# Three attention stages: transposes one block later, a third numerator tile, a joining DMA, and low parts made on GpSimd

## The reference, cut to what matters

```python
# first block: three dilations, joined by their log-sum-exps (one softmax with a mask of counts)
s = einsum('bhrnqe,bhrnke->bhrnqk', qb, kw); s = where(mask, s, NEG_INF)
p = exp(s - max(s)); o = einsum('bhrnqk,bhrnke->bhrnqe', p, vw) / sum(p)
# second block, twice (8 query heads, 2 key heads), then gated
scores = einsum('bqkgd,bskd->bkgqs', qb, k) * scale
y_attn = einsum('bkgqs,bskd->bqkgd', softmax(scores), v) * silu(g_a)
y = concatenate([y_attn, y_conv, y_four]) @ w_out[l]
```

## Time and profile before

| | |
|---|---|
| median of three runs | 3447.35 us |
| profiled execution, its time and its span | 3444.82 us, 3443.0 us |
| busy share of the span: PE, DVE, ACT, POOL | 95%, 60%, 39%, 12% |
| first attention, first scores to first projection matmul | 1203.45 to 1411.67 us |
| second | 2534.60 to 2743.55 us |
| third | 3137.11 to 3344.65 us |

### The profile page before, as it was taken

One profiled execution on the slowest core, in us unless ns is written; L12 is line 12 of the kernel. 1 busy time (PEld: TensorE's weight loads), 2 busy tenths in 40 slices (PEclk: granted clock), 3 DMA queues, 4 the chain that ended last, 5 costly groups with the idle time before them and its releaser, 6 DMA issues. The chain is left out here.

```text
span 3443.0 us, 39579 instructions
## 1 busy us (share of the span) xinstructions
PE 3274.5 (95%) x16006; PEld 2689.4 (78%) x16006; DVE 2076.9 (60%) x2647; ACT 1329.9 (39%) x1996; POOL 404.7 (12%) x505
## 2 busy tenths in 40 slices
PE   5999999999999789999999999899989999998998
PEld 3788888878797678878888888767868887786887
DVE  7555555554764789565655555562259886225986
ACT  4222222232334378432222222552147754214772
POOL 0000011121012112021011101001001200100120
PEclk8999999999998699999999999999999999999999
DMA  5222222226355368312222222224333312433331
GB/s 198 86 90 82 86 86 74 87 73 112 111 196 179 69 88 96 77 37 90 94 98 86 74 89 95 57 73 136 103 81 62 58 41 96 134 105 81 65 55 61
DMA packets 137366, 315.19 MB, mean 92 GB/s; under 512 B 55152, under 2 KB 72304, under 8 KB 126176
## 3 DMA queue, kind: packets, MB, share of 16 engines
q1 hardware_dynamic: 74960, 213.60, 19.6%
q0 software_dynamic: 62224, 99.05, 13.9%
HBM read 261.52 MB, written 51.10 MB: 91 GB/s over the span
## 5 line engine op out<-in xcount | busy, mean ns | idle before, releaser
L2088 DVE TENSOR_TENSOR w_lo<-w_raw,w_hi 128x1024 fp32r<-128x1024 f32 (+1 forms) x131 | 221.9, 1694 | 333.9 <-ACT w_hi L1502 333.9
L848 PE MATMUL psum<-a_hi,w_hi 128*128 128x512 f32 x704 | 276.5, 393 | 5.9 <-DVE a_lo L2210 3.8
L848 PE MATMUL psum<-a_hi,w_lo 128*128 128x512 f32 x704 | 274.9, 391 | 0.0
L848 PE MATMUL psum<-a_lo,w_hi 128*128 128x512 f32 x704 | 274.9, 390 | 0.0
L1256 PEld LDWEIGHTS psum<-mats,attn_num 128*128 128x128 f32 x1536 | 169.6, 144 | 115.4 <-ACT attn_num L1853 89.9
L1844 ACT ACTIVATE attn_th<-psum 128x512 fp32r<-128x512 f32 x384 | 209.6, 597 | 123.9 <-PE psum L1256 117.8
L2563 DVE TENSOR_TENSOR attn_tl<-psum,attn_th 128x512 fp32r<-128x512 f32 x384 | 247.2, 684 | 16.1 <-ACT attn_th L1844 12.1
L1256 PE MATMUL psum<-mats,attn_num 128*128 128x128 f32 x1536 | 215.3, 284 | 39.0 <-ACT attn_num L1853 28.8
L2278 DVE SCALAR_TENSOR_TENSOR x<-psum,cols,x 128x1024 f32<-128x1024 f32 x144 | 184.4, 1282 | 94.8 <-PE psum L848 94.6
L1502 ACT ACTIVATE w_hi<-w_raw 128x1024 fp32r<-128x1024 f32 (+1 forms) x131 | 183.8, 1403 | 143.0 <-PE psum L848 51.1
L2557 DVE TENSOR_REDUCE attn_sm<-psum 128x1 f32<-128x1024 f32 x128 | 156.0, 1220 | 32.0 <-PE psum L1246 31.9
(11 more groups left out here) (567 smaller groups left out, 8446.8 us busy)
## 6 DMA issues: line engine op xcount, KB each, us to landing
w_raw<-in_w_ada SPq DMA_DIRECT2D x52, 1024.0 KB, 5.0
w_raw<-in_w_gu SPq DMA_DIRECT2D x44, 1024.0 KB, 4.9
w_raw<-in_w_in SPq DMA_DIRECT2D x34, 1024.0 KB, 5.1
w_raw<-in_w_down SPq DMA_DIRECT2D x22, 1024.0 KB, 5.0
w_raw<-in_w_out SPq DMA_DIRECT2D x12, 1024.0 KB, 7.9
qk_hi_scratch<-p_out_hi POOLq DMA_DIRECT2D x18, 512.0 KB, 3.0
qk_lo_scratch<-p_out_lo POOLq DMA_DIRECT2D x18, 512.0 KB, 3.8
w_early<-in_w_ada SPq DMA_DIRECT2D x8, 1024.0 KB, 18.2
```

What stands on the lines that cost most here:

```text
L848: mm = e.matmul(bank, a[:, k * width + m * P:k * width + (m + 1) * P], b(k, h), start=(ends[0] and k == order[0] and i == 0), stop=(ends[1 ...
L2088: e.tensor_tensor(like(src, lo), src, like(src, hi.bitcast(F32)), ALU.subtract).then_inc(*w_done.mark(n, part))
```

## The change

1. **One more block in flight.** PE transposes block u-2 in iteration u and not u-1; ACT's `num_high`, DVE's `low_parts` and the product with the values move by one too; the loops run one iteration longer. The first attention gets a third numerator tile and a third tile for the maximum.
2. **The join of result halves.** For z < 14, ACT copies all 128 partitions of the product out of PSUM, and POOL issues an accumulating DMA that adds one half of 64 partitions onto the other (128 KB, SBUF to SBUF). POOL's multiplication reads its result. ACT's next-but-one copy waits for that multiplication, and PE's product waits for the copy and not for DVE's addition. DVE adds only for z = 14 and 15.
3. **Low parts on GpSimd.** The low parts of the first three pairs of heads, of `out1` block 1 and of the two ungated `out2` blocks are subtracted by POOL; ACT rounds those weights in four pieces of 512 columns (u = 16 to 19, and 32 to 35).
4. SP issues the two gated `out2` loads at z = 11 and not at z = 4.

```diff
-        a.sm = rings(f"{name}_sm", 2, [P, 1], F32, scope)
+        a.sm = rings(f"{name}_sm", 2 if between else 3, [P, 1], F32, scope)
-        a.tm = [t.sqh[i][0:64, :] for i in range(2)]
+        a.tm = [t.sqh[i] for i in range(2)]
+        if between is None:
+            a.nu.append(sb(f"{name}_num2", [P, S], F32, scope))
...
+    def low_by_pool(n):
+        return plan[n][3] in (("out1", 1), ("out2", 0, 0), ("out2", 0, 1), ("out2", 1, 0), ("out2", 1, 1))
+    def joined_by_dma(z):
+        return z < A_HEADS * ST // 4 - 2
...
@@ tensor_program, times_v and the loop
-                        e.wait_ge(*res_done.at(name, z - 2))
+                        e.wait_ge(*half_res.at(name, z - 2))
-            for u in range(n + 3):
+            for u in range(n + 4):
-                if 1 <= u < n + 1:
-                    turn_over(u - 1)
-                if u >= 3:
-                    times_v((u - 3) // 2, 1 - u % 2)
+                if 2 <= u < n + 2:
+                    turn_over(u - 2)
+                if u >= 4:
+                    times_v((u - 4) // 2, u % 2)
...
-                        e.wait_ge(*mix_lo.at(name, "ab"[k // 4], k % 4))
+                        e.wait_ge(*(mix_lo.at(name, "b", k % 4) if k // 4 else low_heads(name, k)))
...
@@ scalar_program
+        def high_piece(n, j):
+            if j == 0:
+                e.wait_ge(*landed(n))
...
+            c = slice(j * BLK // 4, (j + 1) * BLK // 4)
+            e.activation(part_split(n, 0)[0][:, c], raw_of(n)[:, c], ACT.Identity)...
         def round_weights(n, part):
+            if low_by_pool(n):
+                return
...
-                    e.wait_ge(*res_done.at(name, z - 2))
-                e.activation(a.tm[z % 2], ps.of[(name, "o")].half[z % 2][64:128, :], ACT.Identity)...
+                    e.wait_ge(*og_scaled.at(name, z - 2))
+                if joined_by_dma(z):
+                    e.activation(a.tm[z % 2], ps.of[(name, "o")].half[z % 2], ACT.Identity)...
...
-            for u in range(n + 4):
-                if u >= 7 and (u - 7) % 4 == 0:
-                    half_result((u - 7) // 4)
-                if 1 <= u < n + 1:
-                    num_high(u - 1)
+            for u in range(n + 5):
+                if u >= 8 and u % 4 == 0:
+                    half_result(u // 4 - 2)
+                if 2 <= u < n + 2:
+                    num_high(u - 2)
...
+                if 16 <= u < 20 and not masked:
+                    high_piece(blocks.index[tag + (0,)], u - 16)
+                if 32 <= u < 36:
+                    high_piece(blocks.index[tag + (1,)], u - 32)
...
@@ vector_program
-                    if u >= 2:
-                        e.wait_ge(*num_turned.at(name, u - 2, 1))
+                    if u >= len(a.nu):
+                        e.wait_ge(*num_turned.at(name, u - len(a.nu), 1))
...
-                if u >= 29 and (u - 29) % 16 == 0 and u < n:
-                    heads_low((u - 29) // 16)
...
@@ gpsimd_program, attention
+                if u >= 8 and u % 4 == 0 and joined_by_dma(u // 4 - 2):
+                    z = u // 4 - 2
+                    own, other = ((slice(0, 64), slice(64, P)), (slice(64, P), slice(0, 64)))[(z // 2) % 2]
+                    e.wait_ge(*half_res.at(name, z))
+                    e.dma_start(a.tm[z % 2][own, :], a.tm[z % 2][other, :], accum_op=ALU.add).then_inc(
+                        *halves_in[z % 2].mark(name, z))
                 if u >= 12 and u % 4 == 0:
...
-                    e.wait_ge(*res_done.at(name, z))
+                    e.wait_ge(*halves_in[z % 2].at(name, z))
                     e.wait_ge(*inv_in[z % 2].at(name, z))
...
-                    e.tensor_tensor(part, part, a.rs[z % 2][64 * hh:64 * hh + 64, :], ALU.mult)...
+                    e.tensor_tensor(part, a.tm[z % 2][of, :], a.rs[z % 2][of, :], ALU.mult)...
...
+                if u >= 32 and (u - 32) % 16 == 0 and u <= n:
+                    pp = (u - 32) // 16
+                    e.wait_ge(*og_scaled.now())
+                    e.wait_ge(*mix_hi.at(mix, "a", pp))
+                    e.tensor_tensor(m.mixa[1][:, pp, :], a.og[pp % 2][:], m.mixa[0][:, pp, :].bitcast(F32),
+                                    ALU.subtract).then_inc(*heads_lo.mark(mix, pp))
+                if u == 22 and gated:
+                    low_weights((tag[0], tag[1], 0))
+                if u == 38:
+                    low_weights(tag + (1,))
+        def low_weights(tag):
+            n = block_at(tag)
+            hi, lo = part_split(n, 0)
+            e.wait_ge(*og_scaled.now())
+            e.wait_ge(*w_hi.at(n, 0))
+            e.tensor_tensor(lo, raw_of(n), hi.bitcast(F32), ALU.subtract).then_inc(*w_low.mark(n))
...
@@ sync_program, attention
-                if gated and z == 4:
+                if gated and z == 11:
                     weights(first_block(("out2", i - 1, 0)) + 2 * RAW)
```

More of the change, by code:

```diff
@@ L688, in program_of @@
     og_scaled, og_gated, summed_g = (signal(n, "Pool") for n in ("og_scaled", "og_gated", "summed_g"))
+    w_low, heads_lo = (signal(n, "Pool") for n in ("w_low", "heads_lo"))
+    halves_in = loaded("halves_joined", "POOL", 2)
     const_in, x_in = signal("const_in", "SP", 16), loaded("x_in", "SP", 2)
@@ L787, in halves_of, with block_at, split_done, low_heads @@
         return part_split(n, 0)
+    def low_by_pool(n):
+        return plan[n][3] in (("out1", 1), ("out2", 0, 0), ("out2", 0, 1), ("out2", 1, 0), ("out2", 1, 1))
+    def block_at(tag):
+        return next(b for b, entry in enumerate(plan) if entry[3] == tag)
+    def split_done(n):
+        return w_low.at(n) if low_by_pool(n) else w_done.at(n)
+    def low_heads(mix, pp):
+        return heads_lo.at(mix, pp) if pp < A_HEADS // 2 - 1 else mix_lo.at(mix, "a", pp)
+    def joined_by_dma(z):
+        return z < A_HEADS * ST // 4 - 2
     def with_sums(n, part):
@@ L1493, in scalar_program @@
         blocks = Blocks(plan, lambda n, part: round_weights(n, part), lambda layer, i: None)
+        def high_piece(n, j):
+            if j == 0:
+                e.wait_ge(*landed(n))
+                if part_before[n, 0] is not None:
+                    e.wait_ge(*tile_done.at("block", *part_before[n, 0]))
+            c = slice(j * BLK // 4, (j + 1) * BLK // 4)
+            e.activation(part_split(n, 0)[0][:, c], raw_of(n)[:, c], ACT.Identity).then_inc(
+                *w_hi.mark(n, 0, *(() if j == 3 else (j,))))
         def round_weights(n, part):
+            if low_by_pool(n):
+                return
             if plan[n][0] == "w":
@@ L1829, in half_result @@
                 if z >= 2:
[L1830 to L1831 removed]
+                    e.wait_ge(*og_scaled.at(name, z - 2))
+                if joined_by_dma(z):
+                    e.activation(a.tm[z % 2], ps.of[(name, "o")].half[z % 2], ACT.Identity).then_inc(*half_res.mark(name, z))
+                else:
+                    e.activation(a.tm[z % 2][0:64, :], ps.of[(name, "o")].half[z % 2][64:128, :],
+                                 ACT.Identity).then_inc(*half_res.mark(name, z))
             def heads_high(pp):
@@ L2573, in results @@
                 e.wait_ge(*half_res.at(name, z))
-                if z % 4 == 0 and pp >= 2:
-                    e.wait_ge(*mix_lo.at(mix, "a", pp - 2))
                 e.tensor_tensor(a.og[pp % 2][64 * hh:64 * hh + 64, (z % 2) * HALF:(z % 2 + 1) * HALF],
-                                ps.of[(name, "o")].half[z % 2][0:64, :], a.tm[z % 2], ALU.add).then_inc(*res_done.mark(name, z))
+                                ps.of[(name, "o")].half[z % 2][0:64, :], a.tm[z % 2][0:64, :], ALU.add).then_inc(*res_done.mark(name, z))
             def heads_low(pp):
@@ L2612, in attention @@
                     ml_drained(e)
-                if u >= 7 and (u - 7) % 4 == 0:
-                    results((u - 7) // 4)
-                if 1 <= u < n + 1:
-                    low_parts(u - 1)
+                if u >= 8 and u % 4 == 0:
+                    if not joined_by_dma(u // 4 - 2):
+                        results(u // 4 - 2)
+                if 2 <= u < n + 2:
+                    low_parts(u - 2)
                 if u >= 4 and u % 4 == 0 and u <= n:
                     inverse_sums(u // 4 - 1)
-                if u >= 29 and (u - 29) % 16 == 0 and u < n:
-                    heads_low((u - 29) // 16)
                 if u == ST:
@@ L3086, in load_mix, with attention @@
                 e.dma_start(m.t[k][:], d.mix[first + k]).then_inc(*mix_in[k].mark(name, k))
-        def attention(name, mix, m, first, n_kv, gated):
+        def attention(name, mix, m, first, n_kv, gated, tag):
             a = m.at
@@ L3179, in block2 @@
             row(m.gain, d.gain[l], "gain", l)
-            attention(at_name, mix, m, 4, 2, True)
+            attention(at_name, mix, m, 4, 2, True, ("out2", l))
             e.wait_ge(*og_gated.now())
```

36 lines of the change are left out of this document (23 added, 13 removed).

## The result

The changed kernel takes 3392.2 us, the median of 4 runs (3388.0 to 3396.5), beside 3448.0 for the kernel before in the same session: a ratio of 0.984, with a 95% interval of 0.9823 to 0.9857. The profiled execution took 3396.5 us (span 3394.7), 48.3 less than that of before.

What follows compares the result with a forecast made beforehand. PE was taken to bound the kernel, waiting each block on ACT's exponential. Savings of 24.7, 22.4 and 17.7 us (64.8), less 6 for keys, gave 59: 3386 from 3444.8, stated as 3387, range 3377 to 3410.

Steps and rivals of the forecast that it cites:

- The ring: Attentions: transposes, high parts, exponential, transposes close a 2.93 us loop (2.96 in the first); an extra block gives 2.82.
- The splits: Five weight-block splits inside the attention loops stop all engines; removing them saves 7.4, 5.2 and about 6 us for three.
- the row that I costed them from: Second attention: three periods around a weight-block split take 16.16 us and not 8.8, so 7.4 us are lost.
- The join: POOL's accumulating DMA of result halves: free if it lands within 19.8 us, as ACT's copy waits for the multiplication.
- my 7 us for it: Gated stages: the accumulating DMA's landing, taken from the nearest load on the same queue, about 7 us.
- by that the join would be free everywhere: All attentions: with a fixed DMA cost of about 2 us, the accumulating DMA would cost nothing.
- Keys of the first attention: Keys take 12.6 us with 11.3 left, so PE waits 1.3 us at four of six loads: 6 us back.
- rival (a): First attention: queue bounds it, keys wait through values, join and multiplication; 19 us in place of 6, 3400; chance 0.22.
- (b): Attentions: period stays at 2.93 us for another reason, only splits and ends go; 3411 us; chance 0.12.
- (c): All attentions: joins land late and ACT's copy waits for POOL; at 25 us landing, 3495 us; chance 0.04.

Runs made afterwards that it cites:

- the undone version: The changed kernel with the weight blocks split by ACT and DVE inside the loop again, out2 loads at z = 4: 3425.7 us, 0.9932.
- block_only: The kernel before plus only the extra block in flight and the third tile: 3417.8 us, 0.9914.
- mult_behind: The changed kernel with first-attention keys issued right behind queries, POOL's multiplications behind the next loads, and pairs' low parts behind them: 3390.5 us, 0.9833.
- k_early: The changed kernel with first-attention keys issued right behind the queries, after the last scores of the head before: 3380.4 us, 0.9808.
- low_behind_keys: The changed kernel with POOL's low parts of head pairs two iterations later in the first attention, behind the key and value loads: 3382.0 us, 0.9814.

## Why the prediction was right, and where it wasn't

*The total.* I forecast 3387 in 3377 to 3410; it is 3392. Of the 48.3 us between the profiled executions, 49.4 lie in the gated stages (forecast 47.1), -0.4 in the first attention (forecast 11.7) and -0.7 elsewhere.

*The ring.* Right in kind: with the extra block PE's idle time is gone, without it the period is 2.93 again. The size was off by 0.07 us, since I took the transposes at 0.85 us from a period that waits; without the wait they start 0.79 apart. That is 4.5 us a stage more. A start of 5.77 us instead of 4.76, another wait of 1.1 us in front of the transposes behind the first and 1.45 us of idle time at the end, for which I had 0.85, gave much of it back: 183.7 and 183.3 where I had 184.2 and 185.1.

*The splits.* Right: the row that I costed them from held, 7.2 and 6.1 us in the undone version, 33 us for all five with 30 in my sum. POOL's subtraction of 128x2048 takes 4.62 us (estimate 4.8) and that of heads 2.41 (2.4). It cost nothing in the gated stages. That it cost nothing in the first was wrong: there it stood ahead of loads.

*The join.* Landing under 19.8 us was right as a condition, and the condition held, narrowly: up to 19.1 us in the first attention, the issue's own 0.9 included (issued 1268.04, multiplication at 1287.18), and ACT waited 0.4 us in all. In the gated stages one wait of a multiplication is put down to a join:

```profile
POOL attn_o L3166 <- DMA sq<-sq: 1.5, 1, 1.5
```

The Trainium skill (DMA: Bandwidth & Descriptors, Latency and other measured facts) puts the fixed cost near 2 us. No run here isolates that cost. The gated stages only bound the landing by the 11 to 13 us from a join to its multiplication (13.2, if the releaser in the line above is right), and my 7 us for it is neither confirmed nor refuted. "by that the join would be free everywhere" was wrong for the first attention: behind keys and values it took 18.6 us, and POOL waited 32.2 us for joins.

*Keys of the first attention: the step that failed.* "From the issue ... 12.6 us in all. So PE waits 1.3 us, at four of the six loads": four of six was right, and 11.3 us left (11.0 measured) too. The landing was not 12.6 but 12.5 to 15.7 us, POOL issued up to 1.1 us late on top of the 0.5 us from product to issue, which the sum had left out, and behind two of the waits PE's clock was at its lower level, for which it had no term: 20.2 us in place of 6. I had written the chain for it down as rival (a), priced at 19, and called it less likely because it "takes the slowest landing that I saw for all six loads". Its price was the nearer one, for another reason than it gave: the odd joins did land about as slowly as that, 14.9 to 19.1 us, but through its chain the keys left only 2.5 us late in all. What grew was the landing of the keys themselves, and it grew with what the change put on POOL and its queue, as `block_only` shows (11.4 and 11.9 us); which part of that, and how, stays open. The Trainium skill (DMA: Bandwidth & Descriptors, Queues, rings and completion order) says that a DMA's semaphore write lands only after every earlier write of its DMA engine; the joins are in line with it, 18.6 us behind keys and values.

So the profiled execution came 10.5 us behind my sum of 3386: 14.2 from this term and 0.7 elsewhere, less 2.1 in the rest of the first attention (188.5 us without its breaks, where I had 190.6) and 2.3 in the gated stages. The median lies 4 us below that execution. So it is partly luck that the total fell inside the narrower forecast: one term was missed by 14 us, and three things that I hadn't foreseen took 8 of them back.

*The rivals.* (a) is answered above. (b) is refuted by the period. (c) didn't come, but `mult_behind` shows its wait.

## What to carry to other kernels

When a pipeline is made one step deeper, everything that is freed at its end is freed a step later: look for loads that wait for the last stage and ask whether their tile is not free earlier (here the keys, read last by the scores, waited for a product). On an engine that both computes and issues DMAs, put loads ahead of work that waits for a landing or takes long, yet not so that this work becomes late for its own reader; each instruction of POOL's program has two deadlines. And price a part by stage and with the order around it: the accumulating DMA was worth 3 us in two stages and cost 11 in the third, where, with the loads moved, the stage took 188.4 us with the joins in it.

## What the hardware showed that was not expected

- A DMA of 128 KB within SBUF, issued behind 1.5 MB of keys and values on POOL's queue, landed in 14.9 to 19.1 us in the four cases in which its landing was waited for.
- Keys of 1 MB landed in 10.6 us or less (heads 2 and 6) or in 12.5 to 15.7 us (the other four) in the change; without the values' loads still up to 13.2, and with neither joins nor low parts on POOL (`block_only`) 11.4 and 11.9 where they were waited for. What decides between the two isn't settled; a load that left at the product and not behind POOL's subtraction was among the shorter once (block 40).
- Keys issued right behind 512 KB of queries took 19.5 us in the one case in which they were waited for (`k_early`, block 48).
- PE's granted clock fell to its lower level behind a wait of 2.08 us in one run (`low_behind_keys`, block 32) and stayed at 1.00 behind one of 3.01 us in another (the change, block 24).
- From the start of eight 128x128 transposes to the start of what follows it is 0.79 us when nothing was waited for, 0.85 in the period of 2.93 us, and 0.92 behind waits of 0.23 and 1.06 us (2547.28 and 2544.95 in the change): a wait costs PE a little more than its length.
